# Expert values of the second layer: weighted activations held in the array, the table streamed in 512 columns

## The reference, cut to what matters

```python
def peer(h, w_q, sub_keys, u_tab, v_tab):
    ...                                    # top 16 of 128*128 experts per head, gate = softmax(score)
    def block(args):
        tb, eb, gb = args
        act = jax.nn.gelu(jnp.einsum('td,thkd->thk', tb, jnp.take(u_tab, eb, axis=0)), approximate=False)
        return jnp.einsum('thk,thkd->td', gb * act, jnp.take(v_tab, eb, axis=0))
    ...
# last layer of second_block:
x = x + mod_x[5] * peer(hx, peer_w_q[i], peer_keys[i], peer_u[i], peer_v[i])
```

## Time and profile before

| | |
|---|---|
| median of 3 runs | 4166.71 us (4164.14 to 4167.09) |
| the profiled execution | 4166.24 us, span of its instructions 4164.4 us |
| TensorE busy | 3772.8 us, 91% of the span |
| VectorE, ScalarE, GpSimd busy | 59%, 35%, 17% |
| matmuls | 22284, each with one weight load |
| mean granted TensorE clock | 0.937 of full speed |

### The profile page before, as it was taken

How to read it: one execution, slowest core, us unless ns; L and a number is a source line. 1 busy time by engine, 2 the same in 40 slices (tenths; PEclk the granted TensorE clock), 3 DMA queues, 4 the chain that set the end, 5 groups by cost and what they waited for, 6 DMA issues and landing times. The chain is left out here.

```text
span 4164.4 us, 58347 instructions
## 1 busy us (share of the span) xinstructions
PE 3772.8 (91%) x22284; PEld 3297.9 (79%) x22284; DVE 2453.1 (59%) x4656; ACT 1469.7 (35%) x1705; POOL 727.9 (17%) x414
## 2 busy tenths in 40 slices
PE   6986789895979999999989999999897988899999
PEld 5986579663757888888778888887766988899999
DVE  5855477737642998777315555554655798404665
ACT  4434143122423234444322222222323445443443
POOL 0100000100001553333330000000000673481000
PEclk9988699887989999999999999998998998899999
DMA  7952056410022434666655567662302546767775
GB/s 291 334 204 93 34 200 244 158 71 21 1 86 78 149 139 147 184 185 173 188 187 218 215 218 255 238 245 93 111 11 102 178 174 177 202 228 254 273 285 209
DMA packets 387378, 713.70 MB, mean 171 GB/s; under 512 B 214529, under 2 KB 267009, under 8 KB 335873
## 3 DMA queue, kind: packets, MB, share of 16 engines
q1 hardware_dynamic: 360896, 616.62, 43.7%
q0 software_dynamic: 21888, 79.70, 5.1%
q10 hardware_dynamic: 4416, 15.05, 0.9%
HBM read 605.40 MB, written 105.91 MB: 171 GB/s over the span
## 5 line engine op out<-in xcount | busy, mean ns | idle before, releaser
L2402 PE MATMUL ps<-arena_split 128*128 128x512 f32 (+1 forms) x6144 | 1069.8, 337 | 21.5 <-DVE arena_split L2375 21.5
L2402 PEld LDWEIGHTS ps<-arena_split 128*128 128x128 f32 x6144 | 948.7, 191 | 142.7 <-issue 20.1
L2192 PE MATMUL ps<-xT_split,arena_split 128*128 128x512 f32 (+1 forms) x4096 | 1025.0, 340 | 30.8 <-ACT arena L2139 17.6
L2172 POOL TENSOR_TENSOR arena_split<-ring,arena_split 128x1024 fp32r<-128x1024 f32 x256 | 645.9, 2528 | 1622.0 <-ACT arena_split L2130 1622.0
L2192 PEld LDWEIGHTS ps<-xT_split,arena_split 128*128 128x128 f32 x4096 | 715.3, 193 | 111.8 <-issue 30.5
L2192 PE MATMUL ps<-hT_split,arena_split 128*128 128x512 f32 (+1 forms) x2048 | 694.1, 339 | 0.0
L2372 DVE TENSOR_TENSOR arena_split<-ring,arena_split 128x2048 fp32r<-128x2048 f32 x128 | 293.3, 2292 | 438.2 <-ACT arena_split L2352 438.2
L273 DVE TENSOR_TENSOR arena_split<-ring,arena_split 128x2048 fp32r<-128x2048 f32 x128 | 292.4, 2291 | 351.9 <-ACT arena_split L267 351.9
L2352 ACT ACTIVATE arena_split<-ring 128x2048 fp32r<-128x2048 f32 x128 | 245.2, 1916 | 712.1 <-PE ps L2402 707.2
L2192 PEld LDWEIGHTS ps<-hT_split,arena_split 128*128 128x128 f32 x2048 | 394.6, 193 | 39.0
L267 ACT ACTIVATE arena_split<-ring 128x2048 fp32r<-128x2048 f32 x128 | 243.7, 1912 | 402.4 <-PE ps L750 155.6
(11 more groups left out here) (253 smaller groups left out, 4659.1 us busy)
## 6 DMA issues: line engine op xcount, KB each, us to landing
ring<-in_weights SPq DMA_DIRECT2D x396, 1024.0 KB, 4.9
arena<-in_side_weights POOLq DMA_DIRECT2D x152, 512.0 KB, 5.6
gates<-arena SPq DMA_DIRECT2D x48, 1024.0 KB, 6.9
activations<-arena SPq DMA_DIRECT2D x128, 256.0 KB, 2.1
arena<-gates SPq DMA_DIRECT2D x64, 512.0 KB, 5.8
arena<-activations SPq DMA_DIRECT2D x64, 512.0 KB, 7.4
activations<-arena SPq DMA_DIRECT2D x128, 128.0 KB, 2.1
arena<-gates SPq DMA_DIRECT2D x64, 256.0 KB, 5.0
```

Source lines behind the costliest of these rows:

```text
L2172: pool.tensor_tensor(low, self.raw(f)[:, j, :], high.bitcast(F32), ALU.subtract)\
L2192: mm = pe.matmul(k.ps[:, j, 0:self.T], self.u[:, 2 * (f % 2) + j, a, t * P:(t + 1) * P], self.h[b][:, t, :], start=n == 0, stop=n == 3 * D ...
L2402: mm = pe.matmul(k.ps[:, t, 0:self.T], self.v[:, f % 2, a, j * D + t * P:j * D + (t + 1) * P], self.weighted[:, f % 2, b, j, :], start=fir ...
```

## The change

In layer two (`self.l` is 1) the operands of the values change places. The weighted activations of 128 tokens are stationary, and the table streams past in 512 columns. 2 blocks x 2 groups of 128 tokens x 3 parts x 2 halves of the 1024 features make 24 matmuls a step. The sum then stands in banks 0 to 3 with tokens on partitions. `PeerAddTurned` takes the place of `PeerAdd` there: ACT and DVE copy two banks each to SBUF, PE turns the 16 tiles of 128x128 into banks 4 to 7, and DVE adds them to `xT` with the same gate as before. Layer one stays as it is.

```diff
+PARTS_BY_TOKENS = ((0, 0), (1, 0), (0, 1))
...
@@ PeerValues.tensor
             pe.wait_ge(k.chunk_products, c + (self.g + 1))
             pe.wait_ge(self.w_low.sem, c + self.w_low.at(1))
+            if self.l:
+                for j in range(2):
+                    for q in range(2):
+                        for n, (a, b) in enumerate(PARTS_BY_TOKENS):
+                            for half in range(2):
+                                at = j * D + half * 512
+                                mm = pe.matmul(k.ps[:, 2 * q + half, :], self.weighted[:, f % 2, b, j, q * P:(q + 1) * P],
+                                               self.v[:, f % 2, a, at:at + 512], start=first(c, 1) and j == 0 and n == 0,
+                                               stop=True, skip_group_check=True)
+                mm.then_inc(self.products.sem, 1)
+                return
...
+class PeerAddTurned(Stage):
+    def scalar(self, act):
+        k = self.k
+        k.enter(act, self.s)
+        for q in range(2):
+            act.activation(self.rows[:, q, 0:512], k.ps[:, 2 * q, :], ACT.Copy).then_inc(self.act_copied.sem, 1)
+
+    def tensor(self, pe):
+        k = self.k
+        k.enter(pe, self.s)
+        for half, copied in enumerate((self.act_copied, self.dve_copied)):
+            pe.wait_ge(copied.sem, copied.at(2))
+            for c in range(4 * half, 4 * half + 4):
+                for q in range(2):
+                    at = c % 2 * SEQ + q * P
+                    mm = pe.transpose(k.ps[:, 4 + c // 2, at:at + P], self.rows[:, q, c * P:(c + 1) * P], k.ident)
+                mm.then_inc(self.turned.sem, 1)
+
+    def vector(self, dve):
+        k = self.k
+        k.enter(dve, self.s)
+        for q in range(2):
+            dve.tensor_copy(self.rows[:, q, 512:D], k.ps[:, 2 * q + 1, :]).then_inc(self.dve_copied.sem, 1)
+        for c in range(DT):
+            dve.wait_ge(self.turned.sem, self.turned.at((c | 1) + 1))
+            last = dve.scalar_tensor_tensor(k.xT[:, c, 0:SEQ], k.ps[:, 4 + c // 2, c % 2 * SEQ:(c % 2 + 1) * SEQ],
+                                            self.gate[:, c:c + 1], k.xT[:, c, 0:SEQ], ALU.mult, ALU.add)
+        last.then_inc(k.stage_done, 1)
...
-            PeerAdd(k, [(a, b, g) for a, b, _, _, g in parts], turn)]
+            PeerAddTurned(k, parts[0][4], 0) if l else PeerAdd(k, [(a, b, g) for a, b, _, _, g in parts], turn)]
```

More of the change, by code:

```diff
@@ L2433, in vector, with __init__ @@
         last.then_inc(k.stage_done, 1)
+class PeerAddTurned(Stage):
+    def __init__(self, k, gate, at):
+        self.k, self.s, self.gate = k, k.stage(), gate
+        self.rows = k.room(at, 2, D)
+        self.act_copied = k.count_of("peer_rows_act", 2)
+        self.dve_copied = k.count_of("peer_rows_dve", 2)
+        self.turned = k.count_of("peer_rows_turned", DT)
+    def scalar(self, act):
[23 more added lines that the diff above has]
+        last.then_inc(k.stage_done, 1)
 def peer_stages(k, l, side=None, turn=None):
```

## The result

| | before | after |
|---|---|---|
| median | 4166.71 us (4160.86 to 4170.27, 5 runs) | 4143.52 us (4140.77 to 4152.39, 5 runs) |
| ratio | | 0.9948 (95% interval 0.9934 to 0.9961) |
| the profiled execution | 4166.24 us | 4140.77 us |

The change makes the kernel faster, by about half a per cent. The forecast was 4149.8 us with a range from 4146 to 4160: the sign and the mechanism came as forecast, and the time lies 2.5 us under the range. How much of the difference belongs to the change is what most of this text is about.

What follows compares the result with a forecast made beforehand. The prediction took TensorE's matmul pace to bound layer two's values. Products -20.6, xT's return +0.95, clock restart +0.75 and the end +1.95 gave -16.95 us, hence 4149.8 us, own range 4147 to 4153, wider 4146 to 4160.

Steps and rivals of the forecast that it cites:

- The bound and the pace: Layer two's values: TensorE bounds them, at 0.120 us a matmul of 256 columns before and 0.2265 us of 512 after.
- The steps' gain: Products of layer two's values: a step goes from 5.76 to 5.44 us, 20.6 us less over 64 steps.
- 512 columns don't pay: Rival for the products: a step stays at 5.76 us and only the end is added, 4168.7 us; chance 3%.
- the bare columns count: Rival for the products: the 0.013 us a matmul vanishes, a step takes 5.15 us, total 4132 us; chance 2%.
- The next in line: Release chain of the table's buffers: its margin shrinks from 0.61 to 0.29 us a step and TensorE remains the bound.
- The transfers: Loads of table and activations in layer two: 289 GB/s at 5.44 us a step, taken to cost nothing.
- The return of xT: The 2 MB transfer in layer two: TensorE's wait grows from 2.00 to 2.95 us, 0.95 more, plus 0.75 for a restart.
- the restart at 1.2 GHz: TensorE after the wait at xT's return: would cost 1.5 us, counted by half as 0.75 us.
- The reading behind the half: TensorE's clock stood after 2.00 us of waiting and had fallen after 4.25; the new wait lies between.
- The end: From the last matmul through copies, transposes and adds: 1.85 us for a later first add plus 0.11, 1.95 us more.
- The sum: All terms for the whole kernel: -20.6 + 0.95 + 0.75 + 1.95 = -16.95 us.
- The step that failed: From sum to time: -16.95 us set on the profiled 4166.24 us gives 4149.3, median 0.47 above, 4149.8 us.

Runs made afterwards that it cites:

- quarters: The changed kernel with each table row block streamed as 256 columns, 48 matmuls a step, tokens still stationary; 4166.05 us, ratio 1.0011 to the kernel before.
- order: The changed kernel with its 24 matmuls a step reordered, halves outside and parts inside; 4146.26 us, ratio 0.9968.
- After_delay: The changed kernel with one more unread ScalarE copy of 128x512 ahead of each high copy of the table in layer two; 4156.90 us, ratio 0.9986.
- After_half: The changed kernel with only the 256 used columns of xT coming back, one transfer of 1 MB instead of 2; 4142.01 us, ratio 0.9954.
- before_look3: The kernel before, unchanged, run once for one more trace; 4159.34 us.
- after_again: The changed kernel, unchanged, run again against the kernel before; 4145.61 us, ratio 0.9962.

## Why the prediction was right or wrong

*The bound and the pace* were right: TensorE, and 0.2265 us a matmul of 512 columns whichever operand streams. The steps' gain came as forecast, 0.32 us each (64 x 0.32 is 20.5; the 20.6 of the prediction is a slip of rounding), and quarters shows that it comes from the number of matmuls. Quarters and order leave nothing of the rivals "512 columns don't pay" and "the bare columns count".

*The next in line* was right, by size too. In the trace VectorE's low part ends 0.34 to 0.40 us before the first matmul that needs it; less the 0.06 us in which TensorE starts, which the forecast counts with the chain, the margin is 0.28 to 0.34 us, for 0.29 forecast. After_delay gives 0.35. The transfers never bound a plain step.

*The return of xT* was mis-sized. The wait was forecast 0.95 us longer and came 1.47 us longer in the first pair: the working took the landing of the transfers as unchanged, and it came 0.51 us later (10.64 us after the issue, not 10.13); why is not shown. Of the restart at 1.2 GHz, which I counted by half, 0.75 us, the whole came: 1.75 us over in the step behind, where before had 0.10. In sum 3.1 us against 1.7. After_half shows the two parts apart: with a short queue there is a wait of 0.33 us and no restart. The reading behind the half, that the clock is kept after 2.00 us of waiting, holds for four of five such waits: before_look3 lost it after 2.28 us. So the kernel before pays the restart in some executions too, and over all traces of the two kernels the change gives back 2.7 us here.

*The end* was right: 1.90 us against 1.85, and 0.11 for the last matmul.

*The sum* was thus -15.3 us in the first pair of traces (-15.6 over all seven) against -16.95 forecast, and after_again's timed difference is -15.8 (-21 to -10 by its interval).

*The step that failed* is the last one of the working, from the sum to a time: "the profiled execution took 4166.24 us ... the median of the runs lies 0.47 above it: 4149.8 us", with an own range of 4147 to 4153 and a lower end of 4146 for all. It set the sum on one execution, and so held everything ahead of the values at the 3783.1 us of that trace. In the changed kernel's trace they start at 3772.9, 10.2 us earlier, and no part of that was in the working. Executions of the kernel before go from 4154.7 to 4171.8 us over 79 runs, with a median of 4162.4; the three given, 4164 to 4167, and the profiled one all lie above it, and their mean is 4.5 us above that of the 44 runs that shared the chip later. With the mean of those 44, 4161.4 us, the same working ends at 4144.5. The spread sits ahead of the changed part, mostly in how soon TensorE's clock rises again in an attention where it waits for others. The first comparison reads 23.2 us between the medians (20.4 between the means), and the change's own part is 15.3. The range had no term for the spread, and it should have been the widest one. The mis-sized return of xT did not cause the miss, it hid some of it by luck: with the measured -15.3 the same step gives 4151.4 us, further off.

What stays open: four of the six traces of kernels with the old order of operands have the slow attention, and none of the eight with the new one. The list of runs hints that the new order doesn't prevent it. The four traces have a mean clock of 0.937 and the other ten 0.939 to 0.941, and among the runs of changed kernels without a trace there are some with the same mark: 4152.56 us at 0.937 in order and 4150.37 at 0.937 in after_half, 11 and 15 us above the fastest of their kernels. But no trace of a changed kernel shows it, and why an execution falls into one group or the other was not found.

## What to carry to other kernels

Where matmuls of 256 columns run back to back, each carries a small cost that is not its columns, and the same columns in half as many matmuls are worth it if an exchange of operands allows 512; measure the pace from starts per window, in both forms. Before such a step is shortened, compare the chain behind the buffers with the new step: here 0.3 us of room was left, and 0.5 us more a step on an engine that is 44% busy cost 12 us. And count, before a forecast of a few tenths of a per cent, how far executions of the unchanged kernel lie apart: a gain on paper of 15 us was measured as 23 and as 16.

## What the runs showed of the hardware that was not expected

- The clock of TensorE after a wait in steady work: at xT's return, four waits of 2.00 to 2.32 us kept it, one of 2.28 us and five of 3.11 to 3.84 us lost it, for about 3 us. Where it was lost, the step behind the wait took 1.4 us (256 columns) to 1.75 us (512) more than a plain one, otherwise 0.1.
- 14 traces of the same attention take three distinct times, 94.3, 98.4 and 101.2 us, with TensorE at 1.2 GHz for about 3, 14 and 20 us of it.
- Halving the matmuls at equal columns removed 0.013 us for each one left out; eight uses in a row of one stationary tile (quarters, 0.120 us a start) removed nothing.
